# Output features of the modulation on VectorE behind the dense stages, latent products of full width, weights in runs of 4 KB

## What is computed

```
ml = split(silu(c) @ ada_w[layer] + ada_b[layer], 6)      # per layer: 6 x 1024 numbers, latent tokens
mc = split(silu(c_ctx) @ ada_w[layer] + ada_b[layer], 6)  # the same for the context tokens
a = modulate(rms_norm(h), shift, scale)                   # h * (1 + scale) + shift
cq, ckv, kpe, gq, gk, gv, gg, glow = split(a @ even_w_in)
q  = rms_norm(cq) @ w_uq        # 8 heads x (64 nope + 32 rope), from 384 latent features
kv = rms_norm(ckv) @ w_ukv      # 8 heads x (64 key + 64 value), from 256 latent features
att = softmax(rope(q) @ [k, rope(kpe)].T / sqrt(96)) @ v
gla = bidirectional gated linear attention over chunks of 64 tokens
h += gate * (concat(att, norm(gla) * silu(gg)) @ w_out)
h += gate * (square(relu(modulate(norm(h)) @ mlp_w1)) @ mlp_w2)
```

## Time and profile before

| | |
|---|---|
| median of 3 runs | 2008.01 us (2003.98 to 2011.1) |
| profiled execution | 2003.37 us, its span 2001.5 us |
| mean granted clock of PE | 0.983 |
| busy: PE, DVE, ACT, POOL | 95%, 52%, 46%, 8% of the span |
| DMA | 252.6 MB in 404800 packets, 42.9% of 16 engines' span |
| input projection of layer 0 | 51.3 to 161.8 us |
| latent projection, turn included | 173.1 to 230.3 us |
| attention, first scores to scan | 233.9 to 326.2 us |
| scan up to the output projection | 326.2 to 396.4 us |
| MLP of layer 0 | 447 to 797 us |

### The profile page before, as it was taken

One profiled execution on the slowest core, in us unless ns is written; L12 is line 12 of the kernel. 1 busy time (PEld: TensorE's weight loads), 2 busy tenths in 40 slices (PEclk: granted clock), 3 DMA queues, 4 the chain that ended last, 5 costly groups with the idle time before them and its releaser, 6 DMA issues.

```text
span 2001.5 us, 39990 instructions
## 1 busy us (share of the span) xinstructions
PE 1897.6 (95%) x16272; PEld 1622.3 (81%) x16272; DVE 1048.1 (52%) x1697; ACT 923.9 (46%) x1490; POOL 154.8 (8%) x151
## 2 busy tenths in 40 slices
PE   6999998999999999998998999999899998989997
PEld 2894345778888887887788899999889998679997
DVE  1421255646423433643455676567676646867654
ACT  2322244334312423535544565447566654457653
POOL 0000000020000001001443100100110001020000
PEclk9999999899999999999999999999999999899999
DMA  7432578433333333322000566655356563226663
GB/s 268 119 118 74 168 221 273 149 84 84 98 101 92 98 95 90 103 74 63 5 4 19 158 176 185 186 146 151 100 144 184 175 184 115 64 75 179 180 177 106
DMA packets 404933, 254.51 MB, mean 127 GB/s; under 512 B 10817, under 2 KB 391361, under 8 KB 404673
## 3 DMA queue, kind: packets, MB, share of 16 engines
q1 hardware_dynamic: 404800, 252.59, 42.9%
HBM read 251.51 MB, written 1.05 MB: 126 GB/s over the span
## 4 chain that ended last, share of the span: by engine, by line
PE 84%; DVE 8%; ACT 4%; issue 2%; DMA 2%; SPq 0%; POOL 0%; ACTq 0%; DVEq 0%; POOLq 0%
PE bank L401 22%; PE bank L403 21%; PE bank L402 21%; PE bank L393 3%; PE bank L626 2%; DMA ring<-ada_w 1%; PE bank L1986 1%; PE bank L420 1%; DVE weights_lo L351 1%; ACT weights_hi L344 1%; DVE h L2613 1%; PE bank L938 1%; PE bank L2011 1%; PE bank L1991 1%; DVE a L2611 1%
## 5 line engine op out<-in xcount | busy, mean ns | idle before, releaser
L401 PE MATMUL bank<-x_hi,weights_hi 128*128 128x256 f32 (+1 forms) x2024 | 643.5, 318 | 27.4 <-DVE x_lo L2569 10.9
L403 PE MATMUL bank<-x_hi,weights_lo 128*128 128x256 f32 (+1 forms) x2024 | 633.8, 313 | 0.0
L402 PE MATMUL bank<-x_lo,weights_hi 128*128 128x256 f32 (+1 forms) x2024 | 633.8, 313 | 0.0
L351 DVE TENSOR_TENSOR weights_lo<-ring,weights_hi 128x1024 fp32r<-128x1024 f32 x376 | 462.0, 1231 | 307.9 <-ACT weights_hi L344 303.7
L344 ACT ACTIVATE weights_hi<-ring 128x1024 fp32r<-128x1024 f32 x376 | 395.9, 1056 | 364.7 <-PE bank L403 352.1
L401 PEld LDWEIGHTS bank<-x_hi,weights_hi 128*128 128x128 f32 x2024 | 388.0, 192 | 60.9 <-issue 22.9
L402 PEld LDWEIGHTS bank<-x_lo,weights_hi 128*128 128x128 f32 x2024 | 388.1, 192 | 23.1 <-issue 1.4
L403 PEld LDWEIGHTS bank<-x_hi,weights_lo 128*128 128x128 f32 x2024 | 387.8, 192 | 22.2
L403 PE MATMUL bank<-hidden_hi,weights_lo 128*128 128x256 f32 (+1 forms) x864 | 271.8, 315 | 0.0
L401 PE MATMUL bank<-hidden_hi,weights_hi 128*128 128x256 f32 (+1 forms) x864 | 271.8, 315 | 0.0
L402 PE MATMUL bank<-hidden_lo,weights_hi 128*128 128x256 f32 (+1 forms) x864 | 271.8, 315 | 0.0
(11 more groups left out here) (356 smaller groups left out, 2118.8 us busy)
## 6 DMA issues: line engine op xcount, KB each, us to landing
ring<-mlp_w SPq DMA_DIRECT2D x128, 512.0 KB, 4.2
ring<-ada_w SPq DMA_DIRECT2D x96, 512.0 KB, 4.6
ring<-w_ffn_in SPq DMA_DIRECT2D x88, 512.0 KB, 3.9
ring<-w_ffn_out SPq DMA_DIRECT2D x32, 512.0 KB, 4.3
ring<-gdn_w_in SPq DMA_DIRECT2D x24, 512.0 KB, 3.9
ring<-even_w_in SPq DMA_DIRECT2D x18, 512.0 KB, 4.5
ring<-w_out SPq DMA_DIRECT2D x16, 512.0 KB, 4.4
ring<-w_in_a SPq DMA_DIRECT2D x14, 512.0 KB, 3.9
```

The lines of the kernel that those rows point to most:

```text
L351: nc.vector.tensor_tensor(w_lo[:, g % AHEAD, :], ring[:, g % RAW, :], w_hi[:, g % AHEAD, :].bitcast(F32), ALU.subtract).then_inc(lo_done[g ...
L401: pe.matmul(dst, lhs[0](k), rhs[0](k), start=start and k == 0, stop=False)
L402: pe.matmul(dst, lhs[0](k), rhs[1](k), start=False, stop=False)
L403: last = pe.matmul(dst, lhs[1](k), rhs[0](k), start=False, stop=stop and k == nk - 1)
```

## The change

Four parts.

**Modulation.** The first 16 tiles stay. The other 80 blocks of 128 features are worked out on DVE. Their weights come feature-major (`ada_t`, 80 x 128 x 1024: the 1024 inputs of an output feature lie in one partition). The two condition vectors are brought to all partitions by a DMA (`cond`, 8 KB read, 1 MB written) and put through Silu there by ACT. For each block DVE multiplies 128x1024 weights with the condition and adds up along the row in the same instruction (`scalar_tensor_tensor` with `accum_out`, L675), once per condition. 32 blocks (`EARLY`) stand behind the `split_lo` of the input projection, behind the squares and behind the ranks; 48 (`LATE`, layer 1's) in the MLP of layer 0, after the first three `split_lo` of each loop body. `Background` is gone, and with it the pieces on PE, the copies on ACT and the turns. Early weights have two buffers, late ones three; SP waits for `mod_used` before it fills one again. ACT starts the attention, and DVE the ranks, only when the blocks before them are counted in `mod_used`. Layer 0's bias is added after the early blocks, layer 1's after the MLP.

**Latent products.** The columns of `w_uq` and `w_ukv` are reordered on the host: two query products hold the 32 rope rows of four heads each, four hold the 64 nope rows of two heads each (18 matmuls for 24); four key products hold two heads each (8 for 16). ACT evicts them in pieces of 32 or 64 rows.

**Layout.** Every weight tile lies in memory with 4 KB in one run per partition; the places are otherwise the same.

**Signals.** Some semaphores are merged, and the load of the delta rule's tables waits for all blocks.

```diff
-        def cols_of(w, c0, n, kb=KB):
-            return w[0:kb * P, c0:c0 + n].rearrange("(k p) c -> p k c", p=P)
-        def dyn(w, c0, r0=0, kb=KB):
-            return w[r0:r0 + kb * P, bass.ds(c0, P)].rearrange("(k p) c -> p k c", p=P)
+        def tile_at(w, n, cols=P):
+            return w[n].rearrange("p (k c) -> p k c", c=cols)
+        def dyn(w, n, r0=0, kb=KB):
+            return w[bass.ds(n, 1), :, r0 * P:(r0 + kb) * P].rearrange("o p (k c) -> (o p) k c", c=P)
...
-        class Background:
...
-            def pe_slot(self, pe, s):
-                for i in range(*self.span(s)):
-                    x, t = self.pieces[i]
-                    x.pe_tile(pe, t)
-                    if i % KB == 3 and i >= KB:
-                        y, g = self.groups[i // KB - 1]
-                        y.pe_turn(pe, g)
-            def act_slot(self, act, s):
-                lo, hi = self.span(s)
-                for n in range(lo // KB, hi // KB):
-                    x, g = self.groups[n]
-                    x.act_copy(act, g)
+        EARLY = NMOD * KB - ADA_A
+        LATE = NMOD * KB
+        PER_BODY = 3
+        mod_here = [sig(f"modulation_here{s}") for s in range(PER_BODY)]
+        mod_used = sig("modulation_used")
+        def conditions(x):
+            return x[:, 0:4, :].rearrange("p (z k) t -> p z (k t)", z=2)
+        def early_w(e):
+            s = e % 2
+            return two_blocks(a, 4 + 2 * s)
+        def late_w(s):
+            if s < 2:
+                return two_blocks(mix, 4 + 2 * s)
+            return tab[:, TURN_AT:TURN_AT + D]
+        def two_blocks(x, k):
+            return x[:, k:k + 2, :].rearrange("p k t -> p (k t)")
+        def dve_features(dve, w, x, to, unread):
+            for z in range(2):
+                ins = nc.vector.scalar_tensor_tensor(out=(unread, w)[z], in0=w, scalar=1.0, in1=conditions(x)[:, z, :],
+                                                     op0=ALU.mult, op1=ALU.mult, accum_out=to(z))
+            ins.then_inc(mod_used.sem, 1)
+        def dve_early(dve, e):
+            if e == 0:
+                dve.wait_ge(silu_done.sem, 2)
+            dve.wait_ge(mod_here[e % 2].sem, 16 * (e // 2 + 1))
+            if e > 0:
+                dve.wait_ge(mod_used.sem, e)
+            dve_features(dve, early_w(e), a, lambda z: mod[:, 0, ADA_A + e, z:z + 1], two_blocks(mix, 0 if e < SECOND else 6))
+        EARLY_HERE = (16 * (EARLY // 2), 16 * (EARLY // 2), 32)
+        def dve_late(dve, body, first, s, loop):
+            if loop is None:
+                dve.wait_ge(mod_here[s].sem, EARLY_HERE[s] + 16 * (first + body + 1))
+            else:
+                dve.wait_ge(mod_here[s].sem, after(EARLY_HERE[s] + 16 * (first + 1), loop, 16 / loop[1]))
+            n = EARLY + PER_BODY * first + s
+            dve.wait_ge(mod_used.sem, n + PER_BODY * body if loop is None else after(n, loop, PER_BODY / loop[1]))
+            unread = two_blocks(a, 2) if first < LATE // PER_BODY - 4 else tmp[:, :, :].rearrange("p u t -> p (u t)")
+            dve_features(dve, late_w(s), mix, lambda z: mod[:, 1, bass.ds(body * PER_BODY + (first * PER_BODY + s), 1), z:z + 1]
+                         .rearrange("p o z -> p (o z)"), unread)
+        def sp_conditions(sp, x, n):
+            sp.dma_start(x[:, 0:4, :].rearrange("p k t -> p (k t)"), d["cond"].broadcast_to((P, 2 * D)))\
+                .then_inc(mod_here[2].sem, 16)
+        def act_conditions(act, x, n):
+            act.wait_ge(mod_here[2].sem, 16 * (n + 1))
+            v = x[:, 0:4, :].rearrange("p k t -> p (k t)")
+            nc.scalar.activation(v, v, ACT.Silu).then_inc(silu_done.sem, 1)
...
+        def sp_early(sp, e):
+            if e >= 2:
+                sp.wait_ge(mod_used.sem, e - 1)
+            sp.dma_start(early_w(e), d["ada_t"][e]).then_inc(mod_here[e % 2].sem, 16)
...
         def dve_even_in(dve):
-            for g in range(even_tiles.first + AHEAD, even_end):
-                split_lo(dve, g)
+            dve_early(dve, 0)
+            dve_early(dve, 1)
+            for t in range(AHEAD, even_tiles.n + glow_tiles.n):
+                split_lo(dve, even_tiles.first + t)
+                dve_early(dve, t - 2)
...
+            dve.wait_ge(mod_used.sem, SECOND)
...
+            for e in range(SECOND, EARLY):
+                dve_early(dve, e)
+            dve_ada(dve, None, 0, ADA_A, EARLY)
...
-            for n in range(MH):
+            for n in range(NQUADS + NPAIRS):
                 if n == 0:
...
-                product(pe, q_lin.bank(n)[0:MQK, :], lambda k: w_uq[:, k, n * MQK:(n + 1) * MQK], lambda k: cqn[:, k, :], QB)\
+                product(pe, q_lin.bank(n)[:, :], lambda k: w_uq[:, k, n * P:(n + 1) * P], lambda k: cqn[:, k, :], QB)\
                     .then_inc(mla_mm.sem, 1)
                 if n == 0:
                     pe.wait_ge(root_done.sem, norm_kv.root + 1)
-                back.pe_slot(pe, n)
...
-                product(pe, kv_lin.bank(n)[0:NOPE, :], lambda k: w_ukv[:, k, n * P:n * P + NOPE], lambda k: ckvn[:, k, :], KVB)\
+                product(pe, kv_lin.bank(n)[:, :], lambda k: w_ukv[:, k, n * P:(n + 1) * P], lambda k: ckvn[:, k, :], KVB)\
                     .then_inc(mla_mm.sem, 1)
-                back.pe_slot(pe, MH + n)
...
-                    back.act_slot(act, n - 1)
+            for n in range(NQUADS + NPAIRS):
                 act.wait_ge(mla_mm.sem, n + 1)
-                nc.scalar.activation(qT[0:MQK, n, :], q_lin.bank(n)[0:MQK, :], ACT.Copy).then_inc(evac_act.sem, 1)
-            for n in range(MH + TB):
-                back.act_slot(act, MH + n - 1)
-                act.wait_ge(mla_mm.sem, MH + n + 1)
-                src, dst = (kv_lin.bank(n)[0:NOPE, :], kT[0:NOPE, n, :]) if n < MH else (kv_lin.bank(n)[:, :], vt[:, n - MH, :])
-                nc.scalar.activation(dst, src, ACT.Copy).then_inc(evac_act.sem, 1)
+                o, m = q_lin.bank(n), n - NQUADS
+                if m < 0:
+                    for x in range(4):
+                        ins = nc.scalar.activation(qT[NOPE:MQK, 4 * n + x, :], o[x * ROPE:(x + 1) * ROPE, :], ACT.Copy)
+                else:
+                    for x in range(2):
+                        ins = nc.scalar.activation(qT[0:NOPE, 2 * m + x, :], o[x * NOPE:(x + 1) * NOPE, :], ACT.Copy)
+                ins.then_inc(evac_act.sem, 1)
...
-            mla.act(act, back)
+            act.wait_ge(mod_used.sem, EARLY)
+            mla.act(act)
...
-        back.plan([1] * MLA_SLOT)
-        back.plan([MLA_PIECES * (i + 1) // 33 - MLA_PIECES * i // 33 for i in range(33)])
-        back.plan([2] * 10)
...
-            for x in (ada_b, ada_c):
-                dve_ada(dve, ada_c.turned(), x.layer, x.j0, x.n)
...
+                    def side(first):
+                        if not late:
+                            return {}
+                        return {"side": lambda i, t, loop: dve_late(dve, i, first, t, loop) if t < PER_BODY else None}
...
+            act_conditions(act, mix, 1)
...
+            dve.wait_ge(silu_done.sem, 3)
+            mlp0.dve(dve, late=True)
+            dve_ada(dve, None, 1, 0, LATE)
...
+                    if g is even_tiles and t == AHEAD + FIRST:
+                        sp.wait_ge(xl_done.sem, n1.lo + KB)
+                        sp_conditions(sp, a, 0)
+                        sp_early(sp, 0)
+                        sp_early(sp, 1)
+                    if g is odd_tiles and t == VB + QKB:
+                        sp.wait_ge(mod_used.sem, EARLY + LATE)
+                        sp.dma_start(turn(1), d["tab1"]).then_inc(loaded.sem, 16)
                     load(t, g.source(t))
+                    nth = t + (even_tiles.n if g is glow_tiles else 0)
+                    if g is even_tiles and t == AHEAD + FIRST:
+                        sp_early(sp, 2)
+                        sp_early(sp, 3)
+                    elif g in (even_tiles, glow_tiles) and nth > AHEAD + FIRST:
+                        sp_early(sp, nth - 4)
...
+                    for e in range(even_tiles.n + glow_tiles.n - 4, EARLY):
+                        sp_early(sp, e)
...
+            act_conditions(act, a, 0)
...
+            for e in range(even_tiles.n + glow_tiles.n - 2, SECOND):
+                dve_early(dve, e)
...
+    features = np.concatenate([ada[0, :, 2 * D:], ada[1]], 1)
+    maps["ada_t"] = np.ascontiguousarray(features.T.reshape(-1, P, D))
```

More of the change, by code:

```diff
@@ L1093, in pe_gla @@
         def pe_gla(pe):
-            def pair(i):
-                back.pe_slot(pe, GLA_SLOT + i)
             for tb in range(TB):
@@ L1132, in pe_gla @@
                 ins.then_inc(G["turned"], 1)
-                pair(4 + q)
             for q in range(2 * GFB):
@@ L1150, in pe_gla @@
                 ins.then_inc(G["updates"], 1)
-                if 1 <= q <= 2:
-                    pair(7 + q)
-            back.pe_end(pe)
             for f in range(GH // 2):
@@ L1179, in act_gla @@
         def act_gla(act):
-            def pair(i):
```

(29 more changed lines are left out.)

195 lines of the change are left out of this document (103 added, 92 removed).

## The result

The changed kernel took 1994.42 us (median of 20 runs, 1986.77 to 2117.71) beside 2005.49 us of the kernel before (20 runs, 1998.72 to 2023.3); the ratio is 0.994, 95% interval 0.992 to 0.9961, so 8 to 16 us came off, not 32. A second set of runs gave 0.9958 (0.9937 to 0.9978). The ratios leave disturbed runs out, the longest of the 20 among them. The mean granted clock of PE, which the profile gives as a share of full speed, fell with the change: 0.957 to 0.969 in the other 19 runs of the changed kernel, 0.979 to 0.988 in 28 of the kernel before in a later set.

What follows compares the result with a forecast made beforehand. PE, busy 1897.6 of 2001.5 us, was taken as the bound. Terms -25.6 - 4 - 4 + 1.8 = -31.8 gave 1971.6 against the profiled 2003.4, 1976 against the median 2008.0; 8-in-10 range 1964 to 1999.

Steps and rivals of the forecast that it cites:

- Latent projection, "I take 25.6": Latent projection: 14 fewer matmuls, 20 pieces and two turns gone from PE save 25.6 us, bounds 22 to 27.
- Attention, "I take 4": Attention: taking out 40 pieces, most of them filling waits for DVE, saves 4 us, bounds 0 to 7.
- Scan, "I take 4": Scan: taking out 20 pieces saves 4 us, with DVE's work on transposed blocks then setting the pace; bounds 1 to 7.
- the clock drops where the pieces were: Attention: PE idles more, half of its 84 us might run at clock 0.5, costing about 12 us: 1988; chance 13%.
- DVE's price, "I take 1.3": Modulation on DVE: one 128x1024 multiply-and-add with a sum costs 1.3 us, 2.6 per block; bounds 1.23 to 2.46.
- The rival on the price: DVE becomes the bound: instruction at 1.8 to 2.09 us, about 1992, chance 5%; over 2.09, slower than before, 9%.
- Tile 4, "1.8 late": Input projection: two blocks ahead on DVE make tile 4's split_lo 1.8 us late for PE, bounds 0 to 8.
- Early and late blocks, "0": Blocks on DVE before the keys' rope (bounds 0 to 6) and in layer 0's MLP (0 to 27) stay hidden: 0.
- loads are late: Feature and condition loads take 8 us instead of 4.5, costing 5 at the start, about 7 before scores: 1988; chance 9%.
- Layout, 0: Weights in runs of 4 KB bring no time, 0 (to -2), as loads already land within their pitch.

Runs made afterwards that it cites:

- no_pieces: The kernel before without the 80 pieces on PE, their loads, copies and turns, their modulation left out and latent products narrow; ratio 1.0027.
- fill_att: The changed kernel with one filler matmul on PE after each unit's transposes in the attention, 33 in all; ratio 0.9879.
- fill_both: The changed kernel with filler matmuls on PE in the attention and also at the scan's places where pieces were; ratio 0.9838, 1969.75 us.
- layout_only: The kernel before with the weight tiles in runs of 4 KB alone, those of `ada_w` excepted; ratio 1.0005.
- wide_only: The kernel before with the wide latent products alone, all 80 pieces staying on PE; ratio 0.9987.

## Why the prediction was wrong

*Latent projection, "I take 25.6": right, in part by luck.* It gave 24.0 and 26.0 in two profiles, with 31.2 us at full clock against 31.6. Two misses make up for each other there: the three groups took 15.9, 7.0 and 7.0 us where the pitches between pieces gave 16.5, 7.4 and 7.6, and the copies on ACT cost a gap of 1.38 that I had not counted.

*Attention, "I take 4", bounds 0 to 7: wrong, and the step that failed.* It was 13 to 16 us slower. The working took a piece to be worth its own length where it is on the path and nothing where it fills a wait, at a clock that stays at 1.00. That clock is the step that failed: without the pieces it was 0.50 for 55 to 61 us in a row, and the pairs of the second half were 5.39 apart instead of 4.11. `no_pieces` shows it by taking the pieces away, `fill_att` by putting fillers in their place. At full clock the term itself holds: 88.2 to 88.5 us with 33 fillers, where 92.3 less 4 is 88.3. With fillers in the scan as well (`fill_both`) the whole is 32 us under the kernel before in the medians of its job, which is the forecast's 31.8. The range is not one chance profile either: the three profiles with pieces have attentions of 92.3 to 94.9, the four without pieces and fillers 104.0 to 108.3.

*Scan, "I take 4", bounds 1 to 7: wrong, by the same step.* It was 4 to 5 us slower. The seven profiles without work in the waits of the scan have 74.0 to 75.8, those with fillers 70.2, 66.2 and 64.1. The profiles with pieces spread over 66.5, 70.3 and 75.1, so the size is less certain than the attention's.

*The rival "the clock drops where the pieces were", 13%, 1988: this is what happened*, but the prediction gave it a low chance and too small a price, and left the scan out. Its price of about 12 for the attention went from "half of it at 0.5", and was 17 to 20 us, against the 88.5 that fillers give: half of it was too little, the whole second half ran at 0.5. The row put up against it, 1662 to 1673 with 6.7 of 11 us busy at full clock, is a short stretch, and said nothing of 84 us of such work in a row. For the attention the traces show the clock with and without work in the waits: 0.50 from 285 to 320 us in the changed kernel, 1.00 from 262 to 297 us with the fillers of `fill_att`. By what rule the clock is granted the runs don't show.

*DVE's price, "I take 1.3": right.* 1.22 us, with 0.08 for the read of the sum in the shadow of the next; two stand 1.14 apart. A block is 2.3 to 2.5. The upper bound of 2.46, twice the row of the plain subtraction, is far off: 160 instructions have a median of 1.22 us, the subtraction of that size 1.23. The rival on the price, which begins at 1.8, falls with it. Its sum has one slip of words: "98.6 + 64 p" is the time on the span's clock at which DVE reaches the keys' rope, not a length from 68.4 on.

*Tile 4, "1.8 late": wrong by about 2 us.* DVE had its low part at 74.45, PE wanted it at 53.14 + 21.8 = 74.9, and its matmuls run on without a gap there. Silu was done at 68.42 with inputs 1.8 later than in the profile of before, so 1.9 us earlier than worked out, and the two blocks took 4.8, not 5.2.

*Early and late blocks, "0": right.* The keys' rope began at 200.43, PE wanted it at 212. In the MLP PE had 1540 records in the window of 350 us, 1538 before, with DVE busy for 257 us of it.

*The rival "loads are late", 9%: no.* The early blocks' loads landed in 3.3 us in the median, the late ones of `mix` in 4.1, the first conditions in 4.6.

*Layout, 0: right,* by the ratio of `layout_only`.

*Behind the scan, not in the prediction:* 10.9 us less in the first profile. Nine profiles of kernels with the features on DVE have 1594.2 to 1605.6 there (mean 1600.8), four of the kernel before and those made from it 1600.7 to 1605.1 (mean 1603.0). So most of the 10.9 is chance; whether about 2 us belong to the change stays open.

The stages of the second profile against the first of before, in the order of the table: +2.2, +0.1, -26.0, 0, +13.3, +3.8, -4.7, in all -11.5 before rounding, within the 8 to 16 of the runs.

## What to carry to other kernels

Before work is taken off PE, look at where it lay. In a chain in which PE alternates with DVE and ACT, work that fills its waits can be what keeps its clock up, and taking it off can cost more than it frees: here the attention's clock was 1.00 from 241 to 320 us with the pieces and 0.50 without them for 61 and 55 us in a row in the two profiles of the changed kernel, and the attention took 13 to 16 us more where 4 less were forecast. Filler can take its place: here a matmul of 0.45 us after every second unit of the attention was enough for all but two drops of 3.4 us. And a kernel that leaves the work out, run before the move is built, tells what the move can gain: here the ratio of 1.0027 without any pieces says that moving them gains nothing as long as nothing takes their place in the waits.

## What the runs showed of the hardware

- In the attention PE's clock was 1.00 with fillers (PE recorded as busy for 34.34 of 44 us, `fill_both`) and 0.50 without them (26.50 of 35 us, 285 to 320 us of the changed kernel), for 61 and 55 us in a row, the start of the scan included, in the two profiles of that kernel. The two shares, 78% and 76%, are alike: at the lower clock the same matmuls are recorded as longer, 1.12 us instead of 0.66 for a group on the values, so the recorded busy time doesn't tell the two apart.
- The drops are not tied to a place alone: the same scan took 70.3 us in the profile of before (drops at 331 and 379 us), 75.1 with 14 matmuls fewer ahead of it on PE (`wide_only`: 317, 341 and 375), and 66.5 with the layout changed only (`layout_only`: 336 and 384).
- One multiply-and-add of 128x1024 with a sum out costs DVE what a plain subtraction of that size does, 1.22 us beside 1.23; the record of the sum's read, 0.08 us, lies beside the next instruction.
